# Weight slots that stay, a reordered tail of the hidden sets, and two roundings moved to GpSimd, in a one-layer encoder step

## The reference, cut to what matters

```python
h = _layer_norm(ALPHA * h + (mix @ w_out + b_out), ln1_g, ln1_b)
f = jnp.square(jax.nn.relu(h @ w_mlp1 + b_mlp1)) @ w_mlp2 + b_mlp2
h = _layer_norm(ALPHA * h + f, ln2_g, ln2_b)
```

## Time and profile before

| what | value |
| --- | --- |
| device time, median of 3 runs | 798.79 us (797.29 to 799.19) |
| the profiled execution's own time | 798.34 us |
| its span | 796.6 us |
| PE busy | 776.4 us (97%) |
| DVE, ACT, POOL busy | 519.6 us (65%), 426.8 us (54%), 145.9 us (18%) |
| granted TensorE clock, mean | 0.994 |
| DMA of 512 KB into `raw`, issue to landing, median | SP's loads 3.6 us, POOL's accumulations 6.9 us |

### The profile page before, as it was taken

The page is one execution under the profiler, slowest core; times in us unless marked ns, Lnnn a source line. Parts: engine busy times, 40 slices in busy tenths (PEclk is TensorE's granted clock), DMA queues, the critical chain, the costliest instruction groups (busy, mean ns, idle before and its releaser), DMA issues.

```text
span 796.6 us, 14048 instructions
## 1 busy us (share of the span) xinstructions
PE 776.4 (97%) x5720; PEld 748.6 (94%) x5720; DVE 519.6 (65%) x762; ACT 426.8 (54%) x666; POOL 145.9 (18%) x195
## 2 busy tenths in 40 slices
PE   8999999999999999999999999999999999999995
PEld 7999899999989999999999999998999999999994
DVE  6823344754546476876968979687775887655644
ACT  5633345655646465563655556587336763477324
POOL 2100000472220110006640000000000000000356
PEclk9999999999999999999999999999999999999998
DMA  8632131112111112233112366645666456653203
GB/s 313 261 123 95 58 114 53 54 57 81 53 53 54 53 53 73 88 114 125 58 50 80 80 190 176 163 123 143 186 173 171 130 141 175 173 125 133 80 2 119
DMA packets 27070, 90.57 MB, mean 114 GB/s; under 512 B 2864, under 2 KB 7104, under 8 KB 26624
## 3 DMA queue, kind: packets, MB, share of 16 engines
q1 hardware_dynamic: 22592, 74.26, 27.3%
q0 software_dynamic: 4000, 15.10, 10.3%
q10 hardware_dynamic: 416, 0.33, 0.1%
HBM read 84.84 MB, written 4.85 MB: 113 GB/s over the span
## 4 chain that ended last, share of the span: by engine, by line
PE 80%; DVE 7%; ACT 6%; issue 3%; DMA 3%; DVEq 0%; ACTq 0%; POOL 0%; SPq 0%; POOLq 0%
PE lin L751 8%; PE lin L752 8%; PE lin L753 8%; PE z L1268 6%; PE z L1269 6%; PE z L1270 6%; PE z L1007 3%; DMA raw<-w_sets 3%; PE lin L1145 3%; PE lin L1146 3%; PE lin L1147 3%; PE lin L1285 2%; PE lin L1287 2%; PE lin L1286 2%; PE lin L1268 2%
## 5 line engine op out<-in xcount | busy, mean ns | idle before, releaser
L751 PE MATMUL lin<-h_hi,whi 128*128 128x288 f32 (+1 forms) x448 | 133.8, 299 | 0.0
L752 PE MATMUL lin<-h_lo,whi 128*128 128x288 f32 (+1 forms) x448 | 132.5, 296 | 0.0
L753 PE MATMUL lin<-h_hi,wlo 128*128 128x288 f32 (+1 forms) x448 | 132.0, 295 | 0.0
L751 PEld LDWEIGHTS lin<-h_hi,whi 128*128 128x128 f32 x448 | 84.2, 188 | 1.3 <-issue 1.1
L752 PEld LDWEIGHTS lin<-h_lo,whi 128*128 128x128 f32 x448 | 84.2, 188 | 0.1
L753 PEld LDWEIGHTS lin<-h_hi,wlo 128*128 128x128 f32 x448 | 84.3, 188 | 0.0
L1839 ACT ACTIVATE whi<-raw 128x1024 fp32r<-128x1024 f32 x48 | 50.7, 1056 | 55.4 <-DMA raw<-w_sets 18.0
L2695 DVE TENSOR_TENSOR wlo<-raw,whi 128x1024 fp32r<-128x1024 f32 x48 | 58.7, 1223 | 22.3 <-ACT whi L1839 22.3
L2098 DVE TENSOR_TENSOR wlo<-raw,whi 128x1024 fp32r<-128x1024 f32 x41 | 50.9, 1242 | 28.6 <-ACT whi L1361 26.5
L1361 ACT ACTIVATE whi<-raw 128x1024 fp32r<-128x1024 f32 x38 | 40.0, 1053 | 50.5 <-PE lin L753 32.5
L1268 PE MATMUL z<-f_ops,whi 128*128 128x288 f32 x176 | 52.8, 300 | 3.4 <-DVE f_ops L2764 2.0
(11 more groups left out here) (456 smaller groups left out, 2572.7 us busy)
## 6 DMA issues: line engine op xcount, KB each, us to landing
raw<-w_stream SPq DMA_DIRECT2D x64, 512.0 KB, 3.2
raw<-w_sets SPq DMA_DIRECT2D x48, 512.0 KB, 3.6
raw<-w_sets POOLq DMA_DIRECT2D x24, 512.0 KB, 6.9
w_fifth<-w_sets SPq DMA_DIRECT2D x12, 512.0 KB, 6.2
r<-x_t SPq DMA_DIRECT2D x8, 296.0 KB, 4.4
kcache<-k_cache SPq DMA_DIRECT2D x1, 2048.0 KB, 9.8
vcache<-v_cache SPq DMA_DIRECT2D x1, 2048.0 KB, 8.0
y<-r SPq DMA_DIRECT2D x8, 160.0 KB, 1.8
```

Source lines behind the costliest of these rows:

```text
L751: pe.matmul(out, w_h, hi, start=first, stop=False)
L752: pe.matmul(out, w_h, lo, start=False, stop=False)
L753: return pe.matmul(out, w_l, hi, start=False, stop=last)
```

## The change

The buffers no longer swap (`set_slots` has no argument). The base block of SI of the next set (`load_second`) is loaded as soon as SI of this set has its low part and `x_sum` has read it; AL goes into X's buffer after `dp_sum`; AP's base is loaded before DE. `x_sum` and `dp_sum` move on DVE's list. V6 is no longer stored: V5 + B22 is made in V4's place, ACT rounds it with scale -1, DVE makes its low part with a scalar_tensor_tensor, and then V4 is made in place by subtracting B21. B21 and V4 are rounded by POOL (`v_round`), between its DMA issues, and no longer by ACT. The orders of ACT's and DVE's lists change, and the last unit 0 is worked in the order half 0 without chunks 5 and 7, half 1, then those two.

```diff
-def set_slots(t):
-    return (1, 3, 0, 2, 4) if t % 2 == 0 else (0, 2, 1, 3, 4)
+def set_slots():
+    return 1, 3, 0, 2, 4
-HI_ORDER = (B11, B22, V5, V6, B21, T3, V4)
-LO_ORDER = (B11, V5, V6, B21, T3, B22, V4)
+HI_ORDER = (B11, B22, V5, V6, T3)
+ROUND_ORDER = (B21, V4)
+LO_ORDER = (B11, V5, V6, T3, B21, B22, V4)
...
+            def load_second(t):
+                sp.wait_ge(s_lo, OPS * (t - 1) + W_SI + 1)
+                sp.wait_ge(x_made, t)
+                load_block(t, set_slots()[2], 2, si_base)
+            load_second(1)
             sp.wait_ge(f_lo_done, F_TILES)
...
             for t in range(1, N_SETS):
-                sp.wait_ge(s_lo, o + W_SI + 1)
-                sp.wait_ge(x_made, t)
-                load_block(t, a, 0, al_in)
+                if t > 1:
+                    load_second(t)
                 sp.wait_ge(s_lo, o + W_X + 1)
                 sp.wait_ge(dp_made, t)
-                load_block(t, c, 2, si_base)
+                load_block(t, a, 0, al_in)
                 sp.wait_ge(s_lo, o + W_AP + 1)
+                load_block(t, d, 2, ap_base)
+                sp.wait_ge(s_lo, o + W_DP + 1)
                 load_block(t, b, 1, de_in)
...
+            def first_unit():
+                for h, chunks in ((0, (0, 1, 2, 3, 4, 6)), (1, range(KC)), (0, (5, 7))):
+                    bank, before = out_bank(0, h)
+                    if 0 in chunks:
+                        pe.wait_ge(bank_free[bank], before)
...
-                    if s == 0 and tail is not None:
-                        set_tail(tail, 0)
-                        op_hi(o + 2)
-                        if SETS[tail][1] < 3:
-                            v_hi(tail, V6)
-                            v_hi(tail, B21)
-                        continue
...
+                    if sums:
+                        for f in {0: (V6,), 1: (T3,)}.get(s, ()):
+                            v_hi(tail, f)
+                    if s == 0 and tail is not None:
+                        last_of_set(tail)
+                    if kind == "in" and s in (4, 5):
+                        c = C11 if s == 4 else C22
+                        block_relu(t, c)
+                        block_hi(t, c)
+                        block_plain(t, c)
...
-                    if t == 0 and s < 4:
-                        residual2((4, 0, 2, 6)[s])
-                        residual2((5, 1, 3, 7)[s])
+                    if t == 0 and s in (1, 2, 4, 5):
+                        m = {1: 4, 2: 0, 4: 2, 5: 6}[s]
+                        residual2(m)
+                        residual2(m + 1)
...
                     if inner:
...
+                        elif s == 6:
+                            x_sum(t + 1)
+                            if p < 3:
+                                v_sum(t, V5)
+                                v_sum(t, T3)
                     elif s >= 2:
                         out_add(t, s - 2)
-                    if s == 2:
+                    if sums and s == 2:
+                        v_sum(tail, V4)
+                    op_lo(o + s + 2)
+                    if s == 1:
                         dp_sum(t)
-                    op_lo(o + s + 2)
...
-                        for f in {0: (V6,), 1: (B21, T3), 2: (B22,), 3: (V4,)}.get(s, ()):
+                        for f in {0: (V6,), 1: (T3,), 2: (B21,), 4: (B22, V4)}.get(s, ()):
                             set_lo(tail, f)
...
+            def v_round(t, o):
...
+                if o == B21:
+                    pool.wait_ge(plain_done, 4 * m + 4)
+                else:
+                    pool.wait_ge(v_made, 4 * m + 4)
+                nc.gpsimd.tensor_scalar(f_pairs(o, g, 0), plain_pairs(o, g), 1.0, 0.0, ALU.mult, ALU.add)\
+                    .then_inc(v_rounded, 1)
...
             for t in range(N_SETS):
                 pool.wait_ge(si_base, SET_IN + 16 * (t + 1))
                 pool.dma_start(set_home(c), wsets_d[t, 3], accum_op=ALU.add).then_inc(si_in, 16)
+                if sums:
+                    v_round(t - 2, B21)
                 pool.wait_ge(ap_base, SET_IN + 16 * (t + 1))
                 pool.dma_start(set_home(d), wsets_d[t, 0], accum_op=ALU.add).then_inc(ap_in, 16)
+                if sums:
+                    v_round(t - 2, V4)
```

More of the change, by code:

```diff
@@ L1275, in _, with last_products @@
                     block_product(t, s)
[L1277 to L1282, removed]
+            def last_products(home, m, c, out, between=None):
+                for k in range(KC):
                     moving = f_hi[:, k, c], f_lo[:, k, c]
@@ L1290, in last_products @@
                 return last
+            def first_unit():
+                home = end_home(0)
+                pe.wait_ge(lo_split, U_MLP2 + 1)
+                for h, chunks in ((0, (0, 1, 2, 3, 4, 6)), (1, range(KC)), (0, (5, 7))):
+                    bank, before = out_bank(0, h)
+                    if 0 in chunks:
+                        pe.wait_ge(bank_free[bank], before)
+                    for k in chunks:
+                        pe.wait_ge(f_lo_done, last_ready(k, h))
+                        hi, lo, out = f_hi[:, k, half(h)], f_lo[:, k, half(h)], lin[:, bank, 0:HA]
+                        w_h, w_l = home[0][:, bass.ts(k, P)], home[1][:, bass.ts(k, P)]
+                        pe.matmul(out, w_h, hi, start=k == 0, stop=False, skip_group_check=True)
+                        pe.matmul(out, w_h, lo, start=False, stop=False, skip_group_check=True)
+                        last = pe.matmul(out, w_l, hi, start=False, stop=k == KC - 1, skip_group_check=True)
+                    if KC - 1 in chunks:
+                        last.then_inc(unit_done if h else half_done, 1)
             def sums2(p):
@@ L1321, in _ @@
             pe.wait_ge(relu_done, 8 * sets_before("in", N_SETS) - 2)
-            for m in range(KEPT2):
+            first_unit()
+            for m in range(1, KEPT2):
                 for h in range(2):
@@ L1327, in _ @@
                     pe.wait_ge(bank_free[bank], before)
-                    ready = None if m else (lambda k, h=h: last_ready(k, h))
-                    last_products(end_home(m), m, half(h), lin[:, bank, 0:HA], ready)\
+                    last_products(end_home(m), m, half(h), lin[:, bank, 0:HA])\
                         .then_inc(unit_done if h else half_done, 1)
[L1331 to L1334, removed]
+                    pe.wait_ge(n2_first, h + 1)
+                    pe.matmul(r2_shift(h), ones_2[:, :], first_r2[:, half(h)], start=True, stop=True)\
+                        .then_inc(n2_shift, 1)
             for p, c in enumerate(PARTS2):
@@ L1341, in _ @@
                     ends = p == LAST2 and m == KC - 1
-                    last_products(end_home(m), m, c, lin[:, bank, 0:width2(p)], None, last_sums if ends else None)\
+                    last_products(end_home(m), m, c, lin[:, bank, 0:width2(p)], last_sums if ends else None)\
                         .then_inc(end_done, 1)
@@ L1890, in v_hi @@
                 m = sets_before("in", t)
[L1891 to L1895, removed]
+                act.wait_ge(v_made, 4 * m + (V5, T3, V6).index(o) + 1)
+                nc.scalar.activation(f_pairs(o, g, 0), plain_pairs(V4 if o == V6 else o, g), ACT.Copy,
+                                     scale=-1.0 if o == V6 else 1.0).then_inc(f_hi_done, 1)
             def hs_round(o):
@@ L1946, in _, with last_of_set @@
                 tile(u, 1)
[L1948 to L1958, removed]
+            def last_of_set(t):
+                block_relu(t, C21)
+                if SETS[t][1] == 3:
+                    block_hi(t, C21)
+                block_plain(t, C21)
             for t in range(N_SETS):
@@ L1962, in _ @@
                 tail = t - 1 if t and SETS[t - 1][0] == "in" else None
+                sums = tail is not None and SETS[tail][1] < 3
                 o = OPS * t
                 for s in range(OPS):
[L1965 to L1971 removed]
                     if s == 1:
@@ L1975, in _ @@
                         second_copy(t)
[L1976 to L1979, removed]
                     if t == N_SETS - 1 and s == 6:
@@ L2748, in v_sum @@
                     dve.wait_ge(v_made, 4 * m + 1)
-                    stt(out=plain(V6), in0=plain(V5), scalar=-1.0, in1=plain(B22), op0=ALU.mult,
-                        op1=ALU.subtract).then_inc(v_made, 1)
+                    tt(plain(V4), plain(V5), plain(B22), ALU.add).then_inc(v_made, 1)
                 else:
                     dve.wait_ge(plain_done, 4 * m + 4)
-                    dve.wait_ge(v_made, 4 * m + 3)
-                    stt(out=plain(V4), in0=plain(V6), scalar=-1.0, in1=plain(B21), op0=ALU.mult,
-                        op1=ALU.subtract).then_inc(v_made, 1)
+                    dve.wait_ge(f_lo_done, tiles_before(m) + LO_ORDER.index(V6) + 1)
+                    tt(plain(V4), plain(V4), plain(B21), ALU.subtract).then_inc(v_made, 1)
             def set_lo(t, o):
@@ L2859, in _ @@
                         last_lo(tail, C21)
```

(8 more changed lines are left out.)

67 lines of the change are left out of this document (33 added, 34 removed).

## The result

The changed kernel takes 800.92 us (median of 20 runs, 798.76 to 802.99), the kernel before beside it 797.83 (20 runs, 797.04 to 800.41). The ratio is 1.0033 [1.0025, 1.0042]: 0.33% slower, where the forecast was 795.7 and faster. The profiled execution of the changed kernel took 802.12 (span 800.4, mean granted clock 0.990), that of the kernel before 798.34 (796.6, 0.994). Of these 3.8 us of span, 1.4 lie ahead of set 0, where nothing was changed (its first matmul runs at 455.37 after, at 453.99 before; in the traces of the other seven kernels it lies between these two). From set 0 on the trace is 2.4 longer. The profiled execution of the changed kernel is 1.2 us slower than the median of its 20 runs, whose mean granted clock goes from 0.988 to 0.994.

What follows compares the result with a forecast made beforehand. PE, busy 97% of the span, was taken to bound the kernel, so only gaps and lost clock could return. Removed 9.9, added 6.9, net 3.0 from 798.34, plus 0.45 for the median: 795.7; range 791.5 to 801.0.

Steps and rivals of the forecast that it cites:

- Set 0: Product 0 of set 0: with residuals moved out, ACT's copy no longer binds, X's low part does; a gain of 0.8.
- the pairs of sets 3 and 7: PE's gaps at products 2 and 4, waiting for ACT's copy and DVE's third sum, both go: 2.7 in all.
- unit 0 and 1: The last unit 0 in three pieces gives 1.7, unit 1's new wait takes some 0.85; net 0.85.
- SI's wait: ACT's wait in set 4 for SI's accumulating DMA goes: SI lands by T + 15 (T: set's first matmul), wanted T + 19.3.
- V5's low part of sets 4 and 8 comes at T + 2.6, wanted at T + 3.2: Product 1's gaps go, counted from the set's first matmul (T): 3.7 back in set 4, 1.85 in set 8.
- The wait for B21: Product 3 of sets 4 and 8 waits for B21's low part, moved behind AP's on DVE: 2 x 2.7 = 5.4 added.
- the bare list: DVE's operations through B21's low part, 6.2 behind DE's rounding: B21 at T + 11.7, product 3 waits 2.3.
- Zero to 0.6 late; I take 0.3: GpSimd's rounding of V4, behind the wait for AP's base, reaches DVE late; 0.3 counted inside the 2.6 for B21.
- so I add nothing there: DVE operations beside GpSimd's roundings are not slowed, as one kept its 1.22 beside a blanking; nothing added.
- One case is no rule: 0 to 2 of them, 1.5 each; I take one.: Lower clock behind the two new gaps at product 3 of sets 4 and 8: one drop, 1.5 added.
- Rival (a): New waits eat the gain: 3.3 at both B21 products and half clock behind both, 798.5; chance 0.25.
- Rival (b): Sets 3 and 7: GpSimd's V4 rounding behind a late AP base, product 6 waits 3.4, half clock; 805.5, chance 0.13.

Runs made afterwards that it cites:

- the first experiment: The changed kernel with B21's low part right behind DE's and V4's sum moved earlier on DVE; 792.54 us, ratio 0.9934 against the kernel before.

## Why the prediction was wrong

The net was forecast at 3.0 us faster and the trace has 2.4 slower from set 0 on, 5.4 apart. Three terms make 5.3 of it. By the medians of 20 runs it is 3.1 slower, 6.1 from the forecast; the other 0.7 is not accounted for, and single executions differ by more (1.4 ahead of set 0 alone).

- **Gains: right, but for product 1.** Set 0 gave 0.93 (0.8 forecast), the pairs of sets 3 and 7 went as reckoned, and unit 0 and 1 gave 1.73 less 0.88, the 0.85 forecast. SI's wait went. "V5's low part of sets 4 and 8 comes at T + 2.6, wanted at T + 3.2" failed: gaps of 0.23 and 0.51 with 0.24 each stayed, 1.2 us. The runs showed V4's late rounding in its place, which also runs beside B22's low part: without it both go.
- **The wait for B21: right in place, mechanism and releaser, too short.** Moved back, B21's low part takes the gap away; the step that failed is what was added to the bare list. Forecast 2 x 2.7 = 5.4, measured 3.29 + 3.21 + 0.48 = 7.0, so 1.6 more and just above its own upper bound of 3.2. The bare list made 2.3. "Zero to 0.6 late; I take 0.3" was 0.85 at V5's sum, and "so I add nothing there" was 0.56 on DE's low part and the 1.43 of B22's. Product 3 itself is due about 0.4 later behind the gap at product 1: 2.3 + 0.85 + 0.56 - 0.4 = 3.3. The two small terms had been put inside the 2.6 or at nothing instead of on top of the 2.3. In the kernel with V4's rounding ahead DE's rounding of set 4 ends at T + 5.64, where T + 5.5 was forecast.
- **The clock: the largest miss in this trace.** "One case is no rule: 0 to 2 of them, 1.5 each; I take one." In the profiled execution both gaps had the lower clock, 1.46 and 2.55, so 4.0, 2.5 more than taken; by the filled gaps it is 3.0 to 3.7, some 1.5 to 2.2 more. That a gap of this length need not have it is true: of the six gaps of 3.2 to 3.4 in three kernels one, the 3.27 above, kept 1.00. But with gaps forecast longer than the only one that was followed by 0.50, one of two was too few.
- **The rivals.** Rival (a), 3.3 at both products and the clock behind both, is what happened; its 798.5 lacks the gaps at product 1 (1.2) and the second drop's larger size (about 1.1). With them it is 800.8. That this meets the median of 800.92 is in part luck: the second drop is that of one execution, and the median of before came out 0.96 lower over 20 runs than over the three that the forecast starts from. Rival (b) did not come in its form: AP's base was handed over at T + 14.5, as reckoned, and product 6 has no gap. But V4's rounding did hold DVE up, as it feared: in the changed kernel as the 1.43 of B22's low part beside it, in the first experiment as an idle 0.86. The price was paid in the next set.
- **What GpSimd does to DVE.** The earlier trace rows has a 1.22 that stayed 1.22 beside a GpSimd operation; here DE's low part goes from 1.23 to 1.78. In the earlier trace rows DVE's operation had begun first. The trace of before also has subtractions that began after a GpSimd operation, on both timelines:

```profile
364.83 0.81 POOL L3173 TENSOR_TENSOR sum<-sum,r 128x288 f32<-128x288 f32 x1 [1.53 <-DVE r L2496]
```

```profile
365.05 1.68 DVE L2113 TENSOR_TENSOR stay_lo<-raw,stay_hi 128x1024 fp32r<-128x1024 f32 x1
```

This one ends 1.09 after the GpSimd operation, as DE's low part ends 1.07 after B21's rounding. So the price put at nothing could have been read before. The Trainium skill (GPSIMD Engine Reference, Key points) says that GpSimd contends with VectorE instructions that have two SBUF inputs; these rows agree for VectorE's side as well, and against the reading of the earlier trace rows in the prediction.

Left open: why the lower clock lasted 6.8 us in set 8, from 651.9 inside the gap to 658.7, and 3.4 in set 4, from 559.7, 1.5 us after the gap, to 563.1; and why it stayed away behind the 3.27. Nor was the new wait of unit 1 mended.

## What to carry to other kernels

On an engine that works through a written order, an operand moved behind others is late by their sum, and that sum is to be compared with when its reader is due before anything else is reckoned; here one move decided the sign. If the reader is TensorE and the gap is as long as one that the trace already shows with a lower clock behind it, the clock is charged for each such gap, as the likely case and not the certain one (five of six here). An engine with idle time is not free help: its waits and its slowing of a neighbour belong on top of the chain that its result enters, and one row in which the neighbour was not slowed does not put that at nothing.

## What the runs showed of the hardware

A subtraction of 1024 columns on DVE, 1.21 to 1.23 by itself, took 1.67 to 2.52 beside a rounding on GpSimd that reads one operand, and 2.29 to 2.44 beside two in a row; one of 576 columns went from 0.75 to between 1.21 and 1.88. Where DVE's was the one that grew, it ended 1.08 (1024 columns) or 0.60 to 0.62 (576) after the rounding, or the second of two, in all 28 cases of five kernels, as if it had waited for the rounding's end. In the two kernels of the changed order that round on ACT alone no DVE operation of the sets took over 1.23. Where DVE's came first and kept its 1.21, the rounding took 1.58 and ended 0.53 after it. Which of the two waits does not follow from the shown starts alone: in the first experiment a low part shown from 618.15 took 2.52 though the rounding beside it starts at 618.58. The rounding of 576 columns is shown 1.00 long on GpSimd and two in a row 1.64, where 0.70 was reckoned from 512 columns; ACT does it in 0.69.

The granted clock fell to 0.50 at PE gaps of 1.99 and of 3.2 to 3.4 (five of six), and stayed at 1.00 behind gaps of 1.14 and 1.43, behind one of 3.27, and where gaps of this kind were filled with matmuls. A fall cost 1.5 to 2.6 us.
